# Expert outputs scattered into x itself, with the experts visited in an order that alternates groups

## The chip, the cores and the metric

The kernel runs on one core of a Trainium2 chip. The metric is the device time of one execution in microseconds (us). One profiled execution stands beside the timed runs; every duration in this document is from it.

## The reference, cut to what matters

The model has two layers. Each is a token mixer (gated linear attention in the first, an RG-LRU block in the second) and then a mixture of experts, each added to `x`; a final RMSNorm follows. `x` has 2048 rows (tokens) of 1024 float32 values. There are 32 experts in 4 groups of 8. A token picks one group and then two experts inside it:

```
g_sel = jnp.argmax(grp_logits, axis=-1)
exp_logits = jnp.take_along_axis(exp_logits, g_sel[:, None, None], axis=1)[:, 0]
top_p, top_e = lax.top_k(exp_prob, MOE_TOPK)                  # MOE_TOPK = 2
eid = g_sel[:, None] * MOE_EXPERTS_PER_GROUP + top_e
...
def expert_block(args):
    xblk, e = args
    return (jax.nn.silu(xblk @ w_gate[e]) * (xblk @ w_up[e])) @ w_down[e]
yb = yb * buf_w[:, None].astype(yb.dtype)
out = jnp.zeros((n_tok + 1, d), yb.dtype).at[buf_tok].add(yb)[:n_tok]
```

So each token receives the weighted outputs of two experts of one group. The rows that an expert gets are cut into blocks of 128, the last one padded.

## The kernel before

All five engines run one program, stage after stage: `gla`, `route0` (output projection, residual into the DRAM tensor `x1`, norm, routing, lists of tokens per expert), `experts0`, `lru`, `route1` (the same into `x2`), `experts1`, `finish`. Every float32 matmul is split into a high and a low float32r part (`matmul3`, three matmuls); ScalarE (ACT) makes the high part, VectorE (DVE) the low part, of weights and of activations.

**The expert stages.** The program loops over the 32 experts and, inside, over an expert's blocks (`Fori(0, n)`, n read from a register); g counts blocks over the whole stage. The software pipeline of block g is spread over iterations:

- GpSimd (POOL), L1350 to L1360, in iteration g: gather half 0 of the rows of h for block g+1, store y of the pipeline index g-1, gather half 1 of block g+1, copy a column of the lists. All gathers and scatters are indirect DMAs issued by POOL and go through one queue (q0, "software_dynamic"), and each is preceded by a small copy that names its rows.
- TensorE (PE), `each` from L1526: the gate and up product of block g, first half (12 matmuls); transposes of half 0 of block g+1 (L1497); the second half; transposes of half 1; then `down(g+1)`, which multiplies the activations made one iteration earlier, so y of index i belongs to block i-2; then the transposes of the activation of block g (L1505).
- ACT, L1426: copies the transposed activation (L1388), takes y out of PSUM with the token's weight as scale (L1396, `take_y`), takes half 0 of the next rows (L1383), silu (L1432), half 1.
- DVE, L1480: the low parts of the same (L1461, L1456), and silu times up (L1485).
- Before an expert's first block ACT and DVE split the gate and up weights of expert e+1 (L1404, L1445, four parts) and the down weights of expert e (L1410, L1451). The sync engine (SP) loads 3 MB of weights for each expert two experts ahead (L1290), released by these splits.

There is one buffer `y` and one pair of PSUM banks for it. So `take_y(i)` waits until the scatter of y(i-1) has landed, the scatter of y(i) waits for `take_y(i)`, and `down(i+1)` waits for `take_y(i)`. The scatter writes the 128 rows of y to `y_rows`, a DRAM tensor with two rows per token (and 128 spare rows, the target of padding). Padded slots of a gather read some row of h.

**The stages after.** `lru` first makes x + y_a + y_b for each tile of 128 tokens (`combine`, two DVE adds, L1885 and L1886), stores it back to `x1`, and then takes mean square, root, norm (L1782, L1787, L1890, L1892), transposes and splits. Four tiles are made ahead of its first step, the others one per step. `finish` does the same adds (L2104, L2105) on `x2`, the norm (L2085, L2089, L2107, L2110) and stores to `out`. Their first tiles of x (two and six) are loaded during the expert stage.

## Time and profile before

| | us |
|---|---|
| median of 3 runs | 3018.33 (3016.26 to 3020.65) |
| the profiled execution | 3014.33 |
| its span (first to last instruction) | 3012.6 |
| PE busy | 2619.9 (87%) |
| DVE busy | 1820.9 (60%) |
| ACT busy | 1647.7 (55%) |
| POOL busy | 590.5 (20%) |

The busy times are sums over stages with different limits. PE is marked busy while matmuls are pipelined, so its share says little by itself; the idle time before an instruction, and what ended it, says more. The two expert stages fill about a third of the span. The mean DMA rate over the span is 190 GB/s.

A row of the windows view gives the stretch in us, its length, the busy time and the instruction count of PE, PEld (weight load), DVE, ACT and POOL, the granted TensorE clock as a share of full speed, the DMA engines' busy share, and GB/s. A row of the timeline gives the start, the duration, the engine, the line, the operation, what it writes and reads, and in brackets the idle time of the engine before it and what ended it.

### The profile page before, as it was taken

Reading aid. Unit: us, or ns where it says so; the run is one execution under the profiler, and the core shown is the slowest. Engines: PE = TensorE matmul, PEld = TensorE weight load, DVE = VectorE, ACT = ScalarE, POOL = GpSimd, SP = SyncE. Lnnn points to the kernel's source line nnn. Section 1 sums busy time; section 2 is a strip of 40 time slices with the busy share of each in tenths; the row PEclk is TensorE's granted clock in tenths of the full one; section 3 lists DMA queues with packets and bytes.
Section 4 is the critical chain, followed back from the end, with each engine's and each line's share of the span. In section 5 each row is a group of like instructions: output and inputs, shape, how many; then the busy total and the mean of one; then the engine's idle time right before and its main releaser. Section 6 shows DMA issues by size and latency. Waiting matters only on the chain. (4 is left out here: it accounts for less than half of the span.)

```text
span 3012.6 us, 41660 instructions
## 1 busy us (share of the span) xinstructions
PE 2619.9 (87%) x12246; PEld 2100.4 (70%) x12246; DVE 1820.9 (60%) x3169; ACT 1647.7 (55%) x2260; POOL 590.5 (20%) x795
## 2 busy tenths in 40 slices
PE   6999999999799599999976999999599589999850
PEld 4878878788688477777755777777488467777640
DVE  4555555554456566565636888877465577556546
ACT  5565565554344366565635666675444376555532
POOL 0000000000011344555430000000011255545420
PEclk9999999999899799999987999999799799999985
DMA  3223223331445589789866545451444599877867
GB/s 122 90 91 101 89 91 105 104 107 57 142 155 167 173 295 312 273 281 323 271 218 215 175 166 168 144 171 63 128 154 147 178 350 337 289 264 265 307 237 293
DMA packets 388258, 573.61 MB, mean 190 GB/s; under 512 B 33408, under 2 KB 304000, under 8 KB 384000
## 3 DMA queue, kind: packets, MB, share of 16 engines
q1 hardware_dynamic: 353104, 457.23, 45.8%
q0 software_dynamic: 32688, 105.99, 9.4%
q10 hardware_dynamic: 2304, 8.39, 0.7%
q8 instruction: 81, 1.33, 0.2%
q14 instruction: 81, 0.66, 0.1%
HBM read 449.32 MB, written 122.22 MB: 190 GB/s over the span
## 5 line engine op out<-in xcount | busy, mean ns | idle before, releaser
L1445 DVE TENSOR_TENSOR experts_gu_lo<-carry_raw,experts_gu_hi 128x1024 fp32r<-128x1024 f32 x256 | 296.6, 1220 | 64.4 <-ACT experts_gu_hi L1404 62.4
L1327 POOL DMA_INDIRECT experts_rows<-h_rows,experts_source_now x194 | 269.8, 1391 | 274.0 <-PE experts_ps L1497 129.3
L118 PE MATMUL experts_ps<-experts_gu_hi,experts_hT_hi 128*128 128x512 f32 x760 | 316.3, 416 | 3.0 <-issue 3.0
L119 PE MATMUL experts_ps<-experts_gu_lo,experts_hT_hi 128*128 128x512 f32 x760 | 300.3, 395 | 0.0
L120 PE MATMUL experts_ps<-experts_gu_hi,experts_hT_lo 128*128 128x512 f32 x760 | 299.9, 395 | 0.0
L1404 ACT ACTIVATE experts_gu_hi<-carry_raw 128x1024 fp32r<-128x1024 f32 x256 | 250.2, 1057 | 52.5 <-DMA carry_raw<-in_moe_w_up 42.8
L1456 DVE TENSOR_TENSOR experts_hT_lo<-experts_ps,experts_hT_hi 128x512 fp32r<-128x512 f32 x194 | 133.2, 687 | 240.6 <-ACT experts_hT_hi L1383 233.6
L963 POOL MEMSET route_empty<- 128x512 int32 x2 | 1.1, 564 | 1322.1 <-POOLq L160 1322.1
L118 PE MATMUL route_ps<-route_w_hi,route_src_hi 128*128 128x512 f32 x512 | 208.6, 407 | 45.7 <-DVE route_src_lo L1029 45.7
L1396 ACT ACTIVATE experts_y<-experts_ps,experts_by_block 128x1024 f32<-128x1024 f32 x99 | 110.6, 1117 | 213.8 <-DMA y_rows<-experts_y,experts_target_now 208.4
L119 PE MATMUL route_ps<-route_w_lo,route_src_hi 128*128 128x512 f32 x512 | 203.4, 397 | 0.0
L120 PE MATMUL route_ps<-route_w_hi,route_src_lo 128*128 128x512 f32 x512 | 203.1, 397 | 0.0
L1497 PE MATMUL experts_ps<-ident,experts_rows 128*128 128x128 f32 x776 | 121.1, 279 | 93.4 <-DMA experts_rows<-h_rows,experts_source_now 90.7
L118 PE MATMUL experts_ps<-experts_wd_hi,experts_aT_hi 128*128 (+1 forms) x396 | 172.1, 435 | 26.8 <-DVE experts_aT_lo L1461 22.7
L1497 PEld LDWEIGHTS experts_ps<-ident,experts_rows 128*128 128x128 f32 x776 | 92.8, 142 | 136.1 <-issue 109.9
L120 PEld LDWEIGHTS experts_ps<-experts_gu_hi,experts_hT_lo 128*128 128x128 f32 x760 | 142.6, 188 | 34.6
L118 PEld LDWEIGHTS experts_ps<-experts_gu_hi,experts_hT_hi 128*128 128x128 f32 x760 | 143.0, 188 | 29.6 <-issue 3.5
L119 PE MATMUL experts_ps<-experts_wd_lo,experts_aT_hi 128*128 (+1 forms) x396 | 161.9, 409 | 0.0
L119 PEld LDWEIGHTS experts_ps<-experts_gu_lo,experts_hT_hi 128*128 128x128 f32 x760 | 143.5, 189 | 25.7
L120 PE MATMUL experts_ps<-experts_wd_hi,experts_aT_lo 128*128 (+1 forms) x396 | 161.3, 407 | 0.0
L1451 DVE TENSOR_TENSOR experts_wd_lo<-ahead_wd_raw,experts_wd_hi 128x2048 fp32r<-128x2048 f32 x64 | 146.7, 2293 | 8.3 <-ACT experts_wd_hi L1410 7.0
L975 POOL DMA_INDIRECT expert_lists<-route_entry,route_place_int x64 | 61.7, 964 | 437.1 <-DVE route_place_int L1094 427.3
(322 smaller groups left out, 6757.1 us busy)
## 6 DMA issues: line engine op xcount, KB each, us to landing
carry_raw<-in_moe_w_gate SPq DMA_DIRECT2D x64, 1024.0 KB
carry_raw<-in_moe_w_up SPq DMA_DIRECT2D x64, 1024.0 KB
ahead_wd_raw<-in_moe_w_down SPq DMA_DIRECT2D x64, 1024.0 KB
gla_w_raw<-in_gla_w_in SPq DMA_DIRECT2D x32, 1024.0 KB, 7.3
ahead_wd_raw<-in_lru_w_in SPq DMA_DIRECT2D x32, 1024.0 KB
gla_w_raw<-in_gla_w_in SPq DMA_DIRECT2D x32, 512.0 KB, 5.1
route_src<-oT_rows SPq DMA_DIRECT2D x32, 512.0 KB
x_rows<-route_x_new SPq DMA_DIRECT2D x32, 512.0 KB, 2.9
```

The costliest lines, as they stand in the source:

```text
L118: nc.tensor.matmul(out, w_hi, x_hi, start=first, stop=False)
L119: nc.tensor.matmul(out, w_hi, x_lo, start=False, stop=False)
L120: return nc.tensor.matmul(out, w_lo, x_hi, start=False, stop=last)
L963: pool.memset(empty[:, :, 1], 0)
L975: pool.indirect_dma_start(lists_out, bass.IndirectOffsetOnAxis(place_int[:, j, c:c + 1].bitcast(U32), 0), entry[:, j, c], None).then_inc(s ...
L1327: pool.indirect_dma_start(rows[:, b], None, h_halves[b], bass.IndirectOffsetOnAxis(source_now[b][:].bitcast(U32), 0))\
L1396: nc.scalar.activation(y[:].rearrange("p (b c) -> p b c", b=2), ps[:, Y:Y + 2], ACT.Copy, scale=by_block[:, bass.ds(i + (LAG - 2), 1), 1]. ...
L1404: nc.scalar.activation(gu_hi[:, slot(e), of_part(c)], gu_raw[:, slot(e), of_part(c)], ACT.Copy)\
L1445: nc.vector.tensor_tensor(gu_lo[:, slot(e), of_part(c)], gu_raw[:, slot(e), of_part(c)], gu_hi[:, slot(e), of_part(c)].bitcast(F32), ALU.s ...
L1451: nc.vector.tensor_tensor(wd_lo[:, slot(e)], wd_raw[:, slot(e)], wd_hi[:, slot(e)].bitcast(F32), ALU.subtract).then_inc(wd_lo_done, 1)
L1456: nc.vector.tensor_tensor(hT_lo[:, of_half(b)], ps[:, HT_ + b].rearrange("p (a c) -> p a c", c=P), hT_hi[:, of_half(b)].bitcast(F32), ALU. ...
L1497: last = nc.tensor.transpose(ps[:, HT_ + b, c * P:(c + 1) * P], rows[:, b, c * P:(c + 1) * P], k.ident[:])
```

## The change

The 32 experts are visited as expert 0 of each group, then expert 1 of each group, and so on (`ORDER`), so that blocks that follow one another belong to other groups, or to the same expert, and have no token in common. That allows y to be added into x in DRAM: for each block POOL gathers the block's rows of x1 (or x2) into a new buffer `acc`, DVE computes `y = ps * weight + acc` in one instruction (now DVE's `take_y`; ACT's is gone), and POOL scatters that back over the same rows. `y_rows` no longer exists. The lists hold the token number; padded slots are out of bounds, and the indirect DMAs of all three kinds leave them out. `lru` and `finish` lose their adds, the loads of y and (`lru`) the store of x; they can no longer load x ahead, `finish` has 8 buffers of x and takes the mean square of tile t+1 ahead of the store of tile t.

POOL has two more instructions in an iteration (a copy and a gather) and another order. In the kernel before, this is its order from the start of an iteration; `source_now` names rows of h, `target_now` rows of `y_rows`:

```order
L1321 COPY experts_source_now<-experts_sources 128x1
L1324 REGISTER_ALU
L1325 ISA
L1327 DMA experts_rows<-h_rows,experts_source_now 128x512
L1338 REGISTER_ALU
L1340 ISA
L1340 COPY experts_target_now<-experts_by_block 128x1
L1345 REGISTER_ALU
L1347 DMA y_rows<-experts_y,experts_target_now 4224x1024
L1321 COPY experts_source_now<-experts_sources 128x1
L1325 REGISTER_ALU
L1327 DMA experts_rows<-h_rows,experts_source_now 128x512
```

And this is the same place now; `acc_now` names rows of x, `x_rows` is x1 or x2:

```order
L1369 COPY experts_acc_now<-experts_by_block 128x1
L1358 REGISTER_ALU
L1359 REGISTER_ALU
L1361 DMA x_rows<-experts_y,experts_target_now 2048x1024
L1376 DMA experts_acc<-x_rows,experts_acc_now 128x1024
L1333 ISA
L1333 COPY experts_source_now<-experts_lists 128x1
L1338 REGISTER_ALU
L1340 DMA experts_rows<-h_rows,experts_source_now 128x512
L1333 COPY experts_source_now<-experts_lists 128x1
L1338 REGISTER_ALU
L1340 DMA experts_rows<-h_rows,experts_source_now 128x512
```

The scatter, once between the two gathers of h, stands ahead of both, with the gather of x right behind it.

On DVE the rows from the splits to the end of a first block were, before:

```order
L1445 TENSOR_TENSOR experts_gu_lo<-carry_raw,experts_gu_hi 128x1024 x4
L1451 TENSOR_TENSOR experts_wd_lo<-ahead_wd_raw,experts_wd_hi 128x2048
L1268 UNCONDITIONAL_BRANCH
L1268 ISA
L1461 TENSOR_TENSOR experts_aT_lo<-experts_ps,experts_aT_hi 128x256
L1455 ISA
L1456 TENSOR_TENSOR experts_hT_lo<-experts_ps,experts_hT_hi 128x512
L1485 TENSOR_TENSOR experts_act<-experts_silu,experts_ps 128x256
L1455 REGISTER_ALU
L1456 TENSOR_TENSOR experts_hT_lo<-experts_ps,experts_hT_hi 128x512
```

and are now:

```order
L1470 TENSOR_TENSOR experts_gu_lo<-carry_raw,experts_gu_hi 128x1024 x4
L1476 TENSOR_TENSOR experts_wd_lo<-ahead_wd_raw,experts_wd_hi 128x2048
L1278 UNCONDITIONAL_BRANCH
L1278 ISA
L1486 TENSOR_TENSOR experts_aT_lo<-experts_ps,experts_aT_hi 128x256
L1491 ISA
L1493 REGISTER_ALU
L1495 ISA
L1495 SCALAR_TENSOR_TENSOR experts_y<-experts_ps,experts_by_block,experts_acc 128x1024
L1480 ISA
L1481 TENSOR_TENSOR experts_hT_lo<-experts_ps,experts_hT_hi 128x512
L1522 TENSOR_TENSOR experts_act<-experts_silu,experts_ps 128x256
```

The new instruction on y stands between the low part of the activation and the low part of the next rows.

The diff, cut to its core (`m.sem` and `m.plain` declarations, signatures and the calls are left out):

```diff
+ORDER = [g * EPG + j for j in range(EPG) for g in range(GROUPS)]
...
-                sp.dma_start(into, w[e:e + 1].rearrange("e (k p) c -> p e k c", p=P)).then_inc(landed, DMA)
+                sp.dma_start(into, w[ORDER[e]:ORDER[e] + 1].rearrange("e (k p) c -> p e k c", p=P)).then_inc(landed, DMA)
...
             def gather(b, g):
                 pool.wait_ge(source_set[b], nth(g))
                 pool.wait_ge(hT_ps_done, nth(2 * g - 2 + b))
                 stand(pool)
                 pool.indirect_dma_start(rows[:, b], None, h_halves[b],
-                                        bass.IndirectOffsetOnAxis(source_now[b][:].bitcast(U32), 0))\
+                                        bass.IndirectOffsetOnAxis(source_now[b][:].bitcast(U32), 0),
+                                        bounds_check=T - 1, oob_is_err=False)\
                     .then_inc(rows_in[b], DMA)
...
                 pool.wait_ge(target_set, nth(i + 2))
                 pool.wait_ge(y_done, nth(i))
                 stand(pool)
-                pool.indirect_dma_start(y_rows, bass.IndirectOffsetOnAxis(target_now[:].bitcast(U32), 0),
-                                        y[:], None).then_inc(y_stored, DMA)
+                pool.indirect_dma_start(x_rows, bass.IndirectOffsetOnAxis(target_now[:].bitcast(U32), 0),
+                                        y[:], None, bounds_check=T - 1, oob_is_err=False).then_inc(y_stored, DMA)
+
+            def name_acc(i):
+                if not (isinstance(i, int) and i == -1):
+                    pool.wait_ge(acc_in, nth_acc(i - 1))
+                pool.wait_ge(listed, nth(i - 2))
+                stand(pool)
+                pool.tensor_copy(acc_now[:].unsqueeze(1), by_block[:, bass.ds(i + (LAG - 2), 1), 0:1])\
+                    .then_inc(acc_set, 1)
+
+            def gather_acc(i):
+                pool.wait_ge(acc_set, nth(i + 1))
+                pool.wait_ge(y_done, nth(i - 1))
+                stand(pool)
+                pool.indirect_dma_start(acc[:], None, x_rows,
+                                        bass.IndirectOffsetOnAxis(acc_now[:].bitcast(U32), 0),
+                                        bounds_check=T - 1, oob_is_err=False).then_inc(acc_in, DMA)
 
             def each(e, b, g, n):
-                last = 1 - (n - b + (SLOTS - 2)) // SLOTS
-                column = (e * SLOTS + b + 1 + last * (SLOTS - 1 - b)) % (E * SLOTS)
+                more = (n - b + (SLOTS - 2)) // SLOTS
+                column = more * (b + (ORDER[e] * SLOTS + 1)) + (1 - more) * (ORDER[(e + 1) % E] * SLOTS)
                 column = nc.s_assert_within(column, min_val=0, max_val=E * SLOTS - 1)
+                name_targets(g - 1)
+                name_acc(g)
+                store_y(g - 1)
+                gather_acc(g)
                 name_rows(0, column, g + 1)
                 gather(0, g + 1)
-                name_targets(g - 1)
-                store_y(g - 1)
                 name_rows(1, column, g + 1)
                 gather(1, g + 1)
                 keep_list(column, g + 1)
...
-            def take_y(i):
-                act.wait_ge(y_ps_done, nth(i))
-                act.wait_ge(y_stored, nth_stored(i - 1))
-                act.wait_ge(listed, nth(i - 2))
-                stand(act)
-                nc.scalar.activation(y[:].rearrange("p (b c) -> p b c", b=2), ps[:, Y:Y + 2], ACT.Copy,
-                                     scale=by_block[:, bass.ds(i + (LAG - 2), 1), 1].bitcast(F32))\
-                    .then_inc(y_done, 1)
-
...
+            def take_y(i):
+                dve.wait_ge(y_ps_done, nth(i))
+                dve.wait_ge(acc_in, nth_acc(i))
+                dve.wait_ge(y_stored, nth_stored(i - 1))
+                dve.wait_ge(listed, nth(i - 2))
+                stand(dve)
+                nc.vector.scalar_tensor_tensor(
+                    out=y[:].rearrange("p (b c) -> p b c", b=2), in0=ps[:, Y:Y + 2],
+                    scalar=by_block[:, bass.ds(i + (LAG - 2), 1), 1].bitcast(F32),
...
             def each(e, b, g, n):
                 take_aT(g)
+                take_y(g)
                 take_rows(g + 1, 0)
...
             def load_x(t):
+                after(sp, h_done, t - 2)
                 sp.dma_start(x[:, t % 2], x_dram[t * P:(t + 1) * P, :]).then_inc(x_in[t % 2], DMA)
 
-            def load_y(t):
-                after(sp, x_done, t - 2)
-                sp.dma_start(y_ab[:, t % 2], y_tiles[t]).then_inc(y_in[t % 2], DMA)
-
-            def store_x(t):
-                after(sp, x_done, t)
-                sp.dma_start(x_dram[t * P:(t + 1) * P, :], x[:, t % 2]).then_inc(x_stored[t % 2], DMA)
-
-            def next_x(t):
-                store_x(t - 2)
-                load_y(t)
-                after(sp, h_done, t - 2)
-                after_dma(sp, x_stored[t % 2], t // 2 - 1)
+            for t in range(GT + 2):
                 load_x(t)
-
-            for t in range(2):
-                load_y(t)
-            next_x(2)
-            for t in range(1, GT):
-                next_x(t + 2)
             after(sp, wx["lo_done"], 0)
             load(wx, 1)
             after(sp, wg["lo_done"], 0)
...
-            def combine(t):
-                j = t % 2
-                after_dma(dve, x_in[j], t // 2)
-                after_dma(dve, y_in[j], t // 2)
-                step(nc.vector.tensor_tensor(x[:, j], x[:, j], y_ab[:, j, 0], ALU.add))
-                nc.vector.tensor_tensor(x[:, j], x[:, j], y_ab[:, j, 1], ALU.add).then_inc(x_done, 1)
...
-            combine(0)
             normalise(0)
             for t in range(GT):
-                combine(t + 1)
                 take_hT(t, 2 * (t % 2))
...
                 gated_input(n)
-                if t + 1 < NT:
-                    combine(t + 1)
                 ratio(n)
...
             for t in range(NT):
-                after(sp, x_done, t - DEPTH)
-                sp.dma_start(y_ab[:, t % DEPTH], y_tiles[t]).then_inc(y_in[t % DEPTH], DMA)
-                late = t + XD - DEPTH
-                if t >= DEPTH and late < NT:
-                    after(sp, h_done, late - XD)
-                    sp.dma_start(x[:, late % XD], x_dram[late * P:(late + 1) * P, :])\
-                        .then_inc(early.x_in[late % XD], DMA)
+                after(sp, h_done, t - XD)
+                sp.dma_start(x[:, t % XD], x_dram[t * P:(t + 1) * P, :]).then_inc(x_in[t % XD], DMA)
...
 
         @block.scalar
         def _(act):
-            for t in range(NT):
+            def mean_square(t):
                 j = t % DEPTH
-                after(act, x_done, t)
+                act.wait_ge(x_in[t % XD], (t // XD + 1) * DMA)
                 after(act, std_done, t - 1)
                 nc.scalar.activation(square[:], x[:, t % XD], ACT.Square, accum_out=ss[:, j:j + 1])\
                     .then_inc(ss_done, 1)
+
+            mean_square(0)
+            for t in range(NT):
+                j = t % DEPTH
                 after(act, h_done, t - DEPTH)
                 after(act, ss_done, t)
                 nc.scalar.activation(std[:, j:j + 1], ss[:, j:j + 1], ACT.Sqrt, bias=k.eps[:, 0:1], scale=1.0 / D)\
                     .then_inc(std_done, 1)
+                if t + 1 < NT:
+                    mean_square(t + 1)
                 after(act, h_done, t)
```

## Rows read from the trace of the kernel before

**Rows 1.** Windows: experts0, start of lru, lru, experts1 (stretch, length, busy times, clock, DMA share, GB/s).
```profile
1021.50:1577.20 555.70, 494.77 (x2288) 389.49 (x2288) 326.91 (x363) 319.99 (x412) 266.25 (x362) 0.96 0.81 276
1577.20:1615.50 38.30, 7.83 (x33) 6.29 (x33) 27.40 (x31) 17.78 (x28) 0.00 (x0) 0.50 0.82 300
1615.50:2110.00 494.50, 469.05 (x2016) 375.07 (x2016) 388.00 (x431) 319.33 (x354) 0.00 (x0) 0.98 0.44 147
2400.00:2915.20 515.20, 461.13 (x2143) 361.95 (x2142) 310.89 (x342) 305.23 (x390) 249.02 (x329) 0.98 0.83 289
```
**Rows 2.** One instruction per block (L1485), experts0 and experts1: count, durations, first and last start.
```profile
L1485 DVE TENSOR_TENSOR experts_act<-experts_silu,experts_ps x49: 405/410/422, 1050.0 to 1558.0; 128x256 f32<-128x256 f32 x49
L1485 DVE TENSOR_TENSOR experts_act<-experts_silu,experts_ps x46: 408/410/424, 2414.9 to 2897.2; 128x256 f32<-128x256 f32 x46
```
**Rows 3.** Timeline, all engines, 1203 to 1226 us: start, duration, engine, idle before and releaser.
```profile
1203.05 0.99 POOL L1347 DMA_INDIRECT y_rows<-experts_y,experts_target_now  x1 [0.87 <-POOL experts_target_now L1340]
1205.11 1.00 POOL L1327 DMA_INDIRECT experts_rows<-h_rows,experts_source_now  x1 [0.86 <-POOL experts_source_now L1321]
...
1211.75 1.11 ACT L1396 ACTIVATE experts_y<-experts_ps,experts_by_block 128x1024 f32<-128x1024 f32 x1 [6.14 <-DMA y_rows<-experts_y,experts_target_now]
...
1212.52 0.65 PE L1497 MATMUL experts_ps<-ident,experts_rows 128*128 128x128 f32 x4 [1.27 <-DMA experts_rows<-h_rows,experts_source_now]
1213.17 0.49 PE L118 MATMUL experts_ps<-experts_wd_hi,experts_aT_hi 128*128 x1
...
1219.09 0.60 PE L1497 MATMUL experts_ps<-ident,experts_rows 128*128 128x128 f32 x4
...
1220.48 2.42 POOL L1327 DMA_INDIRECT experts_rows<-h_rows,experts_source_now  x1 [1.84 <-PE experts_ps L1497]
...
1221.96 0.42 DVE L1461 TENSOR_TENSOR experts_aT_lo<-experts_ps,experts_aT_hi 128x256 fp32r<-128x256 f32 x1
...
1222.82 0.49 PE L118 MATMUL experts_ps<-experts_wd_hi,experts_aT_hi 128*128 x1
```
**Rows 4.** Timeline, start of experts0: the first gather and the transposes that wait for it.
```profile
1028.40 1.03 POOL L1327 DMA_INDIRECT experts_rows<-h_rows,experts_source_now  x1 [0.91 <-POOL experts_source_now L1321]
...
1032.06 1.08 PE L1497 MATMUL experts_ps<-ident,experts_rows 128*128 128x128 f32 x4 [19.31 <-DMA experts_rows<-h_rows,experts_source_now]
```
**Rows 5.** One line (L1892): VectorE's instruction on 128x1024 with a scalar and a second tensor, ns.
```profile
L1892 DVE SCALAR_TENSOR_TENSOR lru_h<-lru_early_x,lru_rstd,lru_early_gain x16: 1283/1285/1286, 1587.7 to 1977.3; 128x1024 f32<-128x1024 f32 x16
```
**Rows 6.** Windows inside one expert of two blocks: 1203 to 1213 and 1217 to 1222 us.
```profile
1203.00:1213.00 10.00, 8.73 (x43) 6.76 (x41) 0.81 (x2) 1.64 (x3) 3.73 (x7) 1.00 0.99 350
1217.00:1222.00 5.00, 5.00 (x25) 4.09 (x24) 4.98 (x5) 4.48 (x5) 3.16 (x4) 1.00 0.20 54
```
**Rows 7.** Timeline, start of lru.
```profile
1582.18 1.22 DVE L1885 TENSOR_TENSOR lru_early_x<-lru_early_x,lru_y_ab 128x1024 f32<-128x1024 f32 x1 [4.72 <-DMA lru_y_ab<-y_rows]
...
1606.18 1.06 ACT L1782 ACTIVATE lru_square<-lru_early_x 128x1024 bf16<-128x1024 f32 x1 [1.83 <-DVE lru_early_x L1886]
```
**Rows 8.** Timeline, end of experts1 and finish.
```profile
2902.42 0.98 POOL L1347 DMA_INDIRECT y_rows<-experts_y,experts_target_now  x1 [3.99 <-ACT experts_y L1396]
2906.01 1.11 ACT L1396 ACTIVATE experts_y<-experts_ps,experts_by_block 128x1024 f32<-128x1024 f32 x1 [4.37 <-DMA y_rows<-experts_y,experts_target_now]
...
2915.20 7.79 SPq L2072 DMA_DIRECT2D finish_y_ab<-y_rows  x5
...
2936.30 0.16 DVE L2107 RECIPROCAL finish_rstd<-finish_std 128x1 f32<-128x1 f32 x1 [1.54 <-ACT finish_std L2089]
...
2937.81 0.37 ACTq L2092 DMA_DIRECT2D out<-finish_h  x1
...
2941.39 0.29 ACT L2089 ACTIVATE finish_std<-finish_ss,eps 128x1 f32<-128x1 f32 x1
2941.72 0.17 DVE L2107 RECIPROCAL finish_rstd<-finish_std 128x1 f32<-128x1 f32 x1 [1.54 <-ACT finish_std L2089]
...
3008.98 0.34 ACTq L2092 DMA_DIRECT2D out<-finish_h  x1
```

113 lines of the change are left out of this document (47 added, 66 removed).

## The prediction

> **What bounds the kernel now.** I read the windows by stage first, then the timeline of a few blocks in an expert stage, then the starts of `lru` and `finish`. In the windows the reader sees that the two expert stages take 555.7 and 515.2 us, with PE busy for 494.8 and 461.1, and DMA at 0.81 and 0.83 of its share [rows 1]. PE is the engine that bounds them, nearly. The instruction that runs once per block gives the count and the pace: 49 blocks, (1558.0 - 1050.0) / 48 = 10.58 us each, and 46 blocks, (2897.2 - 2414.9) / 45 = 10.72 us each [rows 2]. With 32 experts that is 17 and 14 experts of two blocks and 33 of one, if none has three. A block without a stall takes 9.65 us, from the first `down` matmul at 1213.17 to the next at 1222.82 [rows 3]. So about 1 us per block is waiting, and the timeline shows on what: the scatter issued at 1203.05 lands only when ACT takes the next y at 1211.75, 8.7 us later, and the gather issued behind it at 1205.11 releases the transposes at 1212.52, 7.4 us later [rows 3]. At the start of the stage, with nothing else in flight, the first gather took 1032.06 - 1028.40 = 3.7 us to the transposes [rows 4]. The long ones coincide with the weights: DMA is at 0.99 of its share from 1203 to 1213 and at 0.20 from 1217 to 1222 [rows 6]. `lru` has PE busy 469 of 494.5 us, behind a start of 38.3 us in which PE does nearly nothing [rows 1]. `finish`, 2915.2 to 3012.6, is a chain of DVE and ACT [rows 8].
>
> **The expert stages.** Parts: ACT loses its instruction on y; DVE gains one of 1.3 us (1.285 for the same form with SBUF operands [rows 5]; its PSUM operand is not shown in this form, so 1.3 to 1.5); POOL gains a copy and a gather; above all, POOL's order changes. Count from the start of a `down`, 1213.17. DVE first finishes the block before, then splits weights for 6.9 us, then the low part of the activation, which ends at 1221.96 + 0.42 = 1222.38, that is +9.2 [rows 3]. Taking y now follows: it ends at +10.55. `down` of the next block, which PE could begin at +9.65, waits for it: 0.9 us for each of 64 experts, 58 us, is what the DVE part alone costs where nothing else is late.
>
> Next, what is queued behind y. POOL's iteration begins with the scatter, which waits for y; then the gather of x; then the first half of h. From the trace two indirect DMAs that follow one another on POOL are 2.06 us apart (1203.05, 1205.11) and the first comes 0.9 us after its release, so the first half of h is issued at 0.9 + 2 x 2.05 = 5.0 us after y. It was issued ahead of the scatter before, so it did not depend on y at all. It is needed one block later, in the middle of the gate and up product; from those transposes to the next `down` PE takes 1222.82 - 1219.09 = 3.75 us. This closes a loop that spans two blocks: 10.55 (down to y) + 5.0 + L (issue to landing) + 3.75 = 19.3 + L, or (19.3 + L) / 2 per block.
>
> L is not shown for this place: three transfers now stand in the queue, the last is the one that matters. From below it is the undisturbed gather [rows 4], 3.7 us: 11.5 us per block. From above it is the gather behind a scatter while weights load, 7.4: 13.35 us per block. The padded slots, of 95 x 128 = 12160 slots all but 8192, are no longer moved, so a third of the indirect traffic goes and the gather of x takes its place; the sum of bytes stays. I take L = 5.2: the gathers of an expert's first block fall mostly into the quiet stretch, those of its second block, and of single-block experts, into the busy one, and less is queued ahead than in the worst row. That is 12.25 us per block against 10.65, the mean of both stages, times 95: +152 us. The bounds are +81 and +257; the first rival below goes under them.
>
> A further reason against a lower L: the gather issued at 1220.48, beside DVE's split of the down weights, kept POOL for 2.42 us instead of 1.00 [rows 3], and for single-block experts scatter and gathers now fall beside the splits.
>
> The new order mixes experts of popular and unpopular groups, so single-block experts, 3 MB of weights for one block of work, come less in a row. At 350 GB/s [rows 6] the weights of an expert (3.15 MB) take 9.0 us and one block's rows of h and y (1.05 MB) 3.0 us, together 12.0, above the 10.65: such a run is bound by DMA before. Spreading it is worth about 1.3 us for some 8 of 33 single blocks: -10 us. Bounds 0 and -40.
>
> At each stage's end y of the last two blocks is taken in turn. Before, the second comes 3.6 us after the first one's scatter is issued (2902.42, 2906.01) [rows 8]; now a gather is issued between them (2.05) and DVE's instruction is longer; with its wake-up +3 us for each of two stages: +6. The memsets of two more buffers lie in the stage's start, beside the load of the lists; nothing.
>
> **lru.** The first adds begin at 1582.18, 4.9 us after the stage's first load at 1577.3, since 1 MB of y comes first [rows 7]. With the load of x alone I take 3.7 as for the undisturbed gather [rows 4]: -1.2; the two adds of tile 0 are on the chain, 2 x 1.22: -2.4. For tiles 1 and 2 the adds lie beside transposes and splits of the tile before; for tile 3 ACT waits 1.83 us for them at 1606.18 [rows 7], and tile 4's adds delay the last split in the same way, 2.4. Start: -8. In the steady part 11 of 16 tiles' adds remain, 2.45 us each, 27 us of DVE; PE idles 25 us there [rows 1], a part of it for DVE. I take -6, bounds 0 and -20. The stores of x and loads of y go, at a DMA share of 0.44: nothing.
>
> **finish.** A tile takes 2941.72 - 2936.30 = 5.42 us [rows 8]. Without adds, and with the mean square ahead, a tile is: reciprocal to store issued 1.51 (2937.81 - 2936.30), the issue 0.37, root 0.29 and its gap: 2.25 us. DMA then moves 1.05 MB per tile, at 350 GB/s 3.0 us, so transfers bound it: 48 us for 16 tiles and 3.6 for the last store (3008.98 to 3012.6): about 51.5 against 97.4, -46. Bounds: -51 if compute sets it, with its start of 8 us (load 3.7, mean square, table load, root, norm), 15 x 2.25 and a tail of 4; -38 if loads and stores mix at 290 GB/s, the mean of an expert stage.
>
> **Sum.** 3014.3 + 152 - 10 + 6 - 14 - 46 = 3102. The median of the runs is 4 us above the profiled execution; I leave that out: 3102, 2.8% slower.
>
> **Rivals.** First, on the other side: the row gathers land in time. It needs L below about 2 + 0.1, since 19.3 + L = 2 x 10.65 at L = 2.0; or POOL being released earlier, because y of an expert's second block, which has no splits in front of it, is taken some 4 us sooner and empty slots make its transfers short. For it: those second blocks hold few rows, and the y wait, 8.7 us, shrinks if it is mostly queueing. Against it: the only undisturbed gather already takes 3.7. Then the expert stages cost 0 to 40 us, say 15, and the sum is 3014.3 + 15 - 64 = 2965 (64 is 10 + 14 + 46 - 6). It decides from where the loop costs less than 64 us: 11.32 us per block, L = 3.35. The Trainium skill (DMA: Bandwidth & Descriptors, Anatomy of one DMA and Queues, rings and completion order) gives an estimate of 2.0 us plus bytes / 436e3, and engines that take turns between queues, so 2.6 us for half of h however busy the weights' queue; by that rule 10.95 us per block and 2979. The rows at 7.4 and 8.7 us [rows 3] speak against it.
>
> Second: everything behind y lands late, as in the busy rows, with 0.5 MB more ahead of the gather of h: L = 7.4 and more, +257 us, 3207. Single-block experts, half of all, would show it.
>
> Third: the DVE term alone, +58, with L hidden and the rest as summed: 3014 + 58 - 64 = 3008, at the edge of no change.
>
> **Chances.** Forecast 0.55; first rival 0.18; second 0.15; third 0.12, of which half is no change and a third is faster. What a measurement can tell from no change is 0.2%, 6 us. Faster 0.18 + 0.04 = 0.22, within 0.06, slower 0.72. The range that holds the time 8 times in 10 reaches from the upper end of the first rival to near the second: 2985 to 3185; the forecast's own is 3040 to 3160.
>
> **What would show it.** In the profile after: the distance between DVE's silu-times-up instructions, 12.2 us on average if right, 10.7 if the first rival holds; PE's L1497 (transposes of h) waiting for the gather of h, 3 to 4 us in most second blocks, 90 us in total before, 200 or more now; `down` waiting for DVE's y about 0.9 us after a split. `finish` at 50 us with tiles 3 us apart, and `lru`'s first product 30 us after its first load. Wrong would be an expert stage no longer than before, or one whose wait is for weights.

## The result, and the profile after

The changed kernel takes 3205.0 us (median of 4 runs, 3198.5 to 3212.2) against 3017.8 of the kernel before on the same chip: a ratio of 1.062, 95% interval 1.0596 to 1.0644. It is 187 us slower. The forecast said 3102 and a range up to 3185: the direction was right, and so was the place, but the cost was double the forecast's 88 us, and the time lies outside the range. The profiled execution took 3212.2 us (span 3210.5), 197.9 more than the one before. The parts below are of these two executions.

First the windows of the changed kernel: experts0, the start of `lru`, `lru`, experts1. The columns are stretch, length, busy times of PE, PEld, DVE, ACT and POOL, the granted clock, DMA share and GB/s.
```profile
1022.00:1700.00 678.00, 526.63 (x2288) 419.91 (x2288) 389.72 (x414) 272.46 (x361) 330.87 (x468) 0.88 0.66 220
1700.00:1740.00 40.00, 14.92 (x53) 11.95 (x54) 17.73 (x26) 18.69 (x29) 0.00 (x0) 0.53 0.45 145
1740.00:2230.00 490.00, 463.01 (x1996) 370.49 (x1994) 360.29 (x404) 320.75 (x356) 0.00 (x0) 0.99 0.34 111
2510.00:3160.00 650.00, 496.01 (x2150) 395.15 (x2150) 375.06 (x395) 264.54 (x347) 308.88 (x432) 0.87 0.66 224
```
Against [rows 1] the expert stages are 100 and more us longer. PE shows as many matmuls in experts0 (2288) but 32 us more busy time, and its clock fell from 0.96 to 0.88. DMA's share fell from 0.81 to 0.66, and the software queue moved 102.87 MB where it moved 105.99: the added time is not a matter of bytes.

The instruction that runs once per block, in both stages (count, durations in ns, first and last start):
```profile
L1522 DVE TENSOR_TENSOR experts_act<-experts_silu,experts_ps x49: 406/420/423, 1063.1 to 1677.8; 128x256 f32<-128x256 f32 x49
L1522 DVE TENSOR_TENSOR experts_act<-experts_silu,experts_ps x46: 405/420/422, 2544.0 to 3134.5; 128x256 f32<-128x256 f32 x46
```
That is 614.7 / 48 = 12.81 and 590.5 / 45 = 13.12 us per block, against 10.58 and 10.72 [rows 2].

The costliest groups whose idle time changed (busy us, mean ns | idle before, releaser). The first row is the kernel before, the others are the changed kernel:
```profile
L1497 PE MATMUL experts_ps<-ident,experts_rows 128*128 128x128 f32 x776 | 121.1, 279 | 93.4 <-DMA experts_rows<-h_rows,experts_source_now 90.7
...
L1536 PE MATMUL experts_ps<-ident,experts_rows 128*128 128x128 f32 x776 | 138.0, 307 | 258.4 <-DMA experts_rows<-h_rows,experts_source_now 258.4
L120 PE MATMUL experts_ps<-experts_gu_hi,experts_hT_hi 128*128 128x512 f32 x760 | 347.9, 458 | 1.2 <-issue 1.2
...
L1495 DVE SCALAR_TENSOR_TENSOR experts_y<-experts_ps,experts_by_block,experts_acc 128x1024 f32<-128x1024 f32 x99 | 126.7, 1279 | 170.7 <-DMA experts_acc<-x_rows,experts_acc_now 163.0
L120 PE MATMUL experts_ps<-experts_wd_hi,experts_aT_hi 128*128 (+1 forms) x396 | 167.8, 424 | 45.4 <-DVE experts_y L1495 45.4
...
L1361 POOL DMA_INDIRECT x_rows<-experts_y,experts_target_now x103 | 106.4, 1033 | 339.8 <-DVE experts_y L1495 336.0
```
POOL stands at the scatter for 336 us until DVE has y; behind it wait the gathers of h; and PE idles 258 us before the transposes of h, where it was 90.7 before. All but 2 us of the 258 are waits for half 0; before, 49 us were for half 0 and 42 for half 1. `down` waits 45 us for DVE's y, where it waited 26.8 in all.

The table adds up the difference. "First" and "last" are the first and last start of the per-block instruction; the loads are SP's first of `lru` and `finish`.

| part | before | after | difference | forecast |
|---|---|---|---|---|
| both stages, first to last block | 990.3 | 1205.2 | +214.9 | +152 - 10 |
| up to the first block of experts0 | 1050.0 | 1063.1 | +13.1 | 0 |
| experts1, from its first transposes of the activation to its first block | 11.0 | 23.6 | +12.6 | 0 |
| last block to the next stage's first load | 19.3 + 18.0 | 25.1 + 28.0 | +15.8 | +6 |
| `lru`, first load to first product | 38.2 | 30.0 | -8.2 | -8 |
| from there to experts1's first transposes of the activation | 788.4 | 787.5 | -0.9 | -6 |
| `finish`, first load to end | 97.4 | 48.0 | -49.4 | -46 |
| sum | | | +197.9 | +88 |

Now one pair of blocks in the timeline of the changed kernel (start, duration, engine, idle before and releaser):
```profile
1331.77 0.49 PE L120 MATMUL experts_ps<-experts_wd_hi,experts_aT_hi 128*128 x1 [1.00 <-DVE experts_y L1495]
...
1332.35 1.02 POOL L1361 DMA_INDIRECT x_rows<-experts_y,experts_target_now  x1 [4.69 <-DVE experts_y L1495]
...
1333.68 1.03 POOL L1376 DMA_INDIRECT experts_acc<-x_rows,experts_acc_now  x1 [0.31 <-issue]
...
1335.84 1.05 POOL L1340 DMA_INDIRECT experts_rows<-h_rows,experts_source_now  x1 [0.92 <-issue]
...
1341.46 1.28 DVE L1495 SCALAR_TENSOR_TENSOR experts_y<-experts_ps,experts_by_block,experts_acc 128x1024 f32<-128x1024 f32 x1 [5.57 <-DMA experts_acc<-x_rows,experts_acc_now]
1342.39 1.11 PE L1536 MATMUL experts_ps<-ident,experts_rows 128*128 128x128 f32 x4 [4.62 <-DMA experts_rows<-h_rows,experts_source_now]
...
1344.58 0.63 PE L120 MATMUL experts_ps<-experts_gu_hi,experts_hT_hi 128*128 128x512 f32 x1
...
1348.81 0.48 PE L120 MATMUL experts_ps<-experts_wd_hi,experts_aT_hi 128*128 x1
...
1357.88 1.27 DVE L1495 SCALAR_TENSOR_TENSOR experts_y<-experts_ps,experts_by_block,experts_acc 128x1024 f32<-128x1024 f32 x1
1359.46 0.50 PE L120 MATMUL experts_ps<-experts_wd_hi,experts_aT_hi 128*128 x1 [1.02 <-DVE experts_y L1495]
```
The predicted loop is there (`down`, y, gather of half 0 of h behind the scatter and the gather of x, transposes, the next `down`), and its four legs can be read. `down` to the end of y: 1359.15 - 1348.81 = 10.3. End of y to the issue of half 0, from the y before the first `down`, which ended at 1330.19 + 1.27: 4.4. Issue to transposes, 1335.84 to 1342.39: L = 6.55. Transposes to `down`, 1342.39 to 1348.81: 6.4. Together 27.7 us for two blocks, where 24.5 was forecast; most of both stages runs in such pairs, 10.5 and then 16 to 17.7 us from block to block. The pair is a typical one: PE waits over 2 us for half 0 at 41 places, and over these the median of L is 6.6 us and that of the leg from transposes to `down` 5.9. From one such wait to the next are two blocks 24 times, at a median of 27.8 us, and three blocks 12 times, at 36.9, where a block without a wait (9.4) lies between. One leg was missed altogether: in this pair PE took 6.4 us from the transposes to `down`, and not 3.75. Windows of that stretch show why (clock in the third column from the end):
```profile
1331.70:1341.70 10.00, 6.01 (x26) 4.60 (x26) 1.96 (x5) 0.38 (x1) 5.09 (x9) 1.00 1.00 352
1342.30:1348.40 6.10, 6.01 (x16) 4.77 (x17) 1.13 (x2) 0.60 (x1) 3.49 (x5) 0.50 0.47 142
```
After 4.62 us without work PE is granted the lower of its two levels, 1.2 GHz, for these 6 us: its matmuls last 0.63 us and not 0.39.

What the two parts, waiting and clock, are in the stages can be read from windows that reach from first to last block, two of the kernel before and two of the changed one:
```profile
1050.00:1558.00 508.00, 474.55 (x2214) 374.53 (x2213) 307.56 (x345) 302.59 (x392) 250.20 (x337) 0.99 0.85 290
2414.90:2897.20 482.30, 444.11 (x2075) 349.46 (x2074) 300.77 (x332) 293.65 (x377) 240.30 (x316) 0.99 0.86 299
```
```profile
1063.10:1677.80 614.70, 503.83 (x2210) 402.39 (x2209) 366.63 (x391) 257.98 (x345) 305.32 (x430) 0.90 0.69 231
2544.00:3134.50 590.50, 471.51 (x2072) 376.53 (x2071) 355.86 (x376) 251.76 (x332) 283.76 (x400) 0.89 0.68 233
```
Of the +214.9 us, PE stands idle for 158 more (229.9 for 71.7), and is busy for 57 more with the same matmuls. The waits are the larger part; the increase in busy time is the clock's, as far as busy times tell.

The start of experts0 in the timeline, first of the kernel before, then of the changed one, and last the same place in experts1:
```profile
1045.51 0.65 PE L1497 MATMUL experts_ps<-ident,experts_rows 128*128 128x128 f32 x4 [1.60 <-DMA experts_rows<-h_rows,experts_source_now]
```
```profile
1043.76 1.26 POOL L1361 DMA_INDIRECT x_rows<-experts_y,experts_target_now  x1 [0.73 <-POOL experts_acc_now L1369]
1045.33 1.97 POOL L1376 DMA_INDIRECT experts_acc<-x_rows,experts_acc_now  x1 [0.31 <-issue]
...
1049.58 1.04 POOL L1340 DMA_INDIRECT experts_rows<-h_rows,experts_source_now  x1 [0.94 <-POOL experts_source_now L1333]
...
1056.96 1.11 PE L1536 MATMUL experts_ps<-ident,experts_rows 128*128 128x128 f32 x4 [13.26 <-DMA experts_rows<-h_rows,experts_source_now]
...
2537.34 1.11 PE L1536 MATMUL experts_ps<-ident,experts_rows 128*128 128x128 f32 x4 [13.25 <-DMA experts_rows<-h_rows,experts_source_now]
```
The gather of h for the second block is issued behind a scatter and a gather of x; PE waits 13.26 us for it, where it waited 1.60, and 13.25 us in experts1.

And the end of experts1, where the last two y follow one another:
```profile
3142.88 1.01 POOL L1361 DMA_INDIRECT x_rows<-experts_y,experts_target_now  x1 [4.59 <-DVE experts_y L1495]
...
3144.99 1.04 POOL L1376 DMA_INDIRECT experts_acc<-x_rows,experts_acc_now  x1 [0.90 <-POOL experts_acc_now L1369]
...
3149.34 1.28 DVE L1495 SCALAR_TENSOR_TENSOR experts_y<-experts_ps,experts_by_block,experts_acc 128x1024 f32<-128x1024 f32 x1 [7.34 <-DMA experts_acc<-x_rows,experts_acc_now]
3151.49 1.01 POOL L1361 DMA_INDIRECT x_rows<-experts_y,experts_target_now  x1 [5.10 <-DVE experts_y L1495]
3162.52 0.34 SPq L2050 DMA_DIRECT2D finish_x<-x_rows  x1
```
Between these two scatters lie 8.6 us, since y now waits for the landing of old x: it starts 6.5 us after the scatter, where ACT's y came 3.6 us after it [rows 8]. The end has a second part, which the rows above do not show: once its last scatter has landed, POOL runs a DRAIN before the next stage may begin. Its durations at the end of experts0 (min/median/max in ns, of a stretch that holds that one and a short one of 40), before and then now:
```profile
L158 POOLq DRAIN  x2: 40/1766/3492, 1572.8 to 1577.3; - x2
```
```profile
L160 POOLq DRAIN  x2: 40/3932/7825, 1694.0 to 1702.9; - x2
```
It takes 7.83 us and not 3.49, and at the end of experts1 6.84 and not 2.76: 8.4 us more in both. All kernels below that gather x in a stage have the long one at its end (6.8 to 7.8 us), all others, e3 too, the short one. Why is open.

`finish`, one tile to the next, and the last store:
```profile
3175.49 0.36 ACTq L2073 DMA_DIRECT2D out<-finish_h  x1
...
3177.74 0.36 ACTq L2073 DMA_DIRECT2D out<-finish_h  x1
...
3206.57 0.34 ACTq L2073 DMA_DIRECT2D out<-finish_h  x1
```
A tile takes 2.25 us here, and 2.37 on the mean of the 15 steps from the first store at 3170.95 to the last, where it took 5.42 [rows 8].

### The profile page after: what moved, and what is told of

It reads as the page before. It is cut to its first block and busy times, and to the rows that moved or that the text cites. A ratio compares the mean times of both kernels' runs of the same rounds, so it can differ in the third digit from the quotient of the medians.

```text
span 3210.5 us, 42505 instructions
## 1 busy us (share of the span) xinstructions
PE 2686.6 (84%) x12246; PEld 2164.0 (67%) x12246; DVE 1867.2 (58%) x3204; ACT 1555.5 (48%) x2161; POOL 712.2 (22%) x1001
## 3 DMA queue, kind: packets, MB, share of 16 engines
q0 software_dynamic: 47232, 102.87, 9.2%
q8 instruction: 81, 1.33, 0.2%
## 5 line engine op out<-in xcount | busy, mean ns | idle before, releaser
L120 PE MATMUL experts_ps<-experts_gu_hi,experts_hT_hi 128*128 128x512 f32 x760 | 347.9, 458 | 1.2 <-issue 1.2
L121 PE MATMUL experts_ps<-experts_gu_lo,experts_hT_hi 128*128 128x512 f32 x760 | 325.2, 428 | 0.0
L122 PE MATMUL experts_ps<-experts_gu_hi,experts_hT_lo 128*128 128x512 f32 x760 | 324.8, 427 | 0.0
L1420 ACT ACTIVATE experts_hT_hi<-experts_ps 128x512 fp32r<-128x512 f32 x194 | 115.8, 597 | 354.6 <-PE experts_ps L1536 354.5
L1340 POOL DMA_INDIRECT experts_rows<-h_rows,experts_source_now x194 | 229.4, 1182 | 192.5 <-POOL experts_source_now L1333 115.1
L1495 DVE SCALAR_TENSOR_TENSOR experts_y<-experts_ps,experts_by_block,experts_acc 128x1024 f32<-128x1024 f32 x99 | 126.7, 1279 | 170.7 <-DMA experts_acc<-x_rows,experts_acc_now 163.0
L120 PEld LDWEIGHTS experts_ps<-experts_gu_hi,experts_hT_hi 128*128 128x128 f32 x760 | 163.6, 215 | 30.9 <-issue 1.6
L121 PEld LDWEIGHTS experts_ps<-experts_gu_lo,experts_hT_hi 128*128 128x128 f32 x760 | 162.9, 214 | 30.0
L1361 POOL DMA_INDIRECT x_rows<-experts_y,experts_target_now x103 | 106.4, 1033 | 339.8 <-DVE experts_y L1495 336.0
L1459 ACT ACTIVATE experts_silu<-experts_ps 128x256 f32<-128x256 f32 x95 | 36.5, 384 | 276.8 <-PE experts_ps L122 270.1
```

The lines of the kernel that those rows point to most:

```text
L120: nc.tensor.matmul(out, w_hi, x_hi, start=first, stop=False)
L121: nc.tensor.matmul(out, w_hi, x_lo, start=False, stop=False)
L122: return nc.tensor.matmul(out, w_lo, x_hi, start=False, stop=last)
L1340: pool.indirect_dma_start(rows[:, b], None, h_halves[b], bass.IndirectOffsetOnAxis(source_now[b][:].bitcast(U32), 0), bounds_check=T - 1, ...
L1361: pool.indirect_dma_start(x_rows, bass.IndirectOffsetOnAxis(target_now[:].bitcast(U32), 0), y[:], None, bounds_check=T - 1, oob_is_err=Fal ...
L1420: nc.scalar.activation(hT_hi[:, of_half(b)], ps[:, HT_ + b].rearrange("p (a c) -> p a c", c=P), ACT.Copy).then_inc(hT_hi_done, 1)
```

## The experiments

The theory: the time is lost because POOL's gather of half 0 of h stands behind y, with the clock's fall on top. The rivals: the gather of x as such (one more transfer, and y waiting for it), the work on DVE, the bound on the row numbers, the order of the experts. Each kernel was timed against the kernel before in the same batch, and batches differ by up to 4 us, so kernels of different batches are compared by their ratios. In the summary, "stages" is both expert stages, first to last block, and the rest is all other time; both are differences of one profiled execution each to that of before, so a few us of them are scatter (e4 shows +8 us in its execution and nothing in its median).

| kernel | median us | ratio to before, 95% | stages | rest | clock |
|---|---|---|---|---|---|
| after | 3205.0 | 1.0620 [1.0596, 1.0644] | +214.9 | -17.0 | 0.916 |
| e1_half0_first | 3068.0 | 1.0151 [1.0131, 1.0171] | +85.3 | -27.6 | 0.937 |
| e2_both_first | 3231.4 | 1.0694 [1.0676, 1.0712] | +242.6 | -22.9 | 0.913 |
| e3_no_acc_gather | 3108.1 | 1.0294 [1.0277, 1.0311] | +146.1 | -52.5 | 0.933 |
| e8_filler | 3174.9 | 1.0521 [1.0504, 1.0539] | +179.9 | -19.4 | 0.956 |
| e6_acc_ahead | 3049.3 | 1.0109 [1.0092, 1.0126] | +77.6 | -41.9 | 0.948 |
| e4_order_alone | 3018.0 | 1.0006 [0.9997, 1.0016] | +7.5 | +0.6 | 0.943 |
| e5_scatter_first | 3071.7 | 1.0183 [1.0166, 1.0200] | +47.6 | +11.1 | 0.937 |
| e7_y_on_dve | 3028.8 | 1.0047 [1.0032, 1.0061] | +5.2 | +6.7 | 0.945 |
| e9_names_first | 3084.9 | 1.0214 [1.0196, 1.0231] | +107.7 | -35.4 | 0.943 |
| e10_skip_empty | 3031.0 | 1.0047 [1.0030, 1.0064] | +9.3 | +5.3 | 0.946 |
| e11_sum_last_only | 3010.0 | 0.9984 [0.9974, 0.9994] | +32.3 | -41.5 | 0.952 |

**e1_half0_first**, the changed kernel with one gather moved back:
```diff
+                name_rows(0, column, g + 1)
+                gather(0, g + 1)
                 name_targets(g - 1)
                 name_acc(g)
                 store_y(g - 1)
                 gather_acc(g)
-                name_rows(0, column, g + 1)
-                gather(0, g + 1)
```


> The changed kernel, but GpSimd gathers half 0 of the next rows of h ahead of the scatter of y, as before; scatter, gather of x and half 1 follow. Theory (place in GpSimd's order: the gathers of h wait for y): the transposes of half 0 no longer wait about 5 us in every second block, the pace falls from 12.96 us per block to about 11.3, set by the y cycle of scatter, gather of x and VectorE; about 3050 us. Rival (the queue is simply longer with the gather of x in it): the gathers land late wherever they stand, half 1 stalls instead, over 3150 us.

Measured 3068.0, 18 us above the expected 3050: 137 of the 187 us go. The place of one gather is most of the loss. What stays is seen in two groups of its trace, first PE at the transposes, then DVE at y:
```profile
  DMA experts_rows<-h_rows,experts_source_now: 159.7, 62
```
```profile
L1495 DVE SCALAR_TENSOR_TENSOR experts_y<-experts_ps,experts_by_block,experts_acc 128x1024 f32<-128x1024 f32 x99 | 126.8, 1281 | 217.6 <-DMA experts_acc<-x_rows,experts_acc_now 217.4
```
PE waits 160 us for rows of h (258 before the edit), and DVE now 217 for the gather of x (163 before the edit). Told apart by half, the wait for half 0 fell from 256 us to 54, about what it is in the kernel before (49), and that for half 1, which still stands behind y, rose from 2 to 106 (42 in the kernel before). So the theory holds for half 0, and in a small part the rival too: half 1 stalls instead.

**e2_both_first**: both gathers of h ahead of the scatter.
```diff
+                name_rows(0, column, g + 1)
+                gather(0, g + 1)
+                name_rows(1, column, g + 1)
+                gather(1, g + 1)
                 name_targets(g - 1)
                 name_acc(g)
                 store_y(g - 1)
                 gather_acc(g)
-                name_rows(0, column, g + 1)
-                gather(0, g + 1)
-                name_rows(1, column, g + 1)
-                gather(1, g + 1)
```


> The changed kernel, but both halves of the next rows of h are gathered ahead of the scatter of y. Theory (place): neither half waits for y, but the scatter now waits for the transposes that free half 1's buffer, so y comes later than with half 0 alone ahead: between 3030 and 3090 us. Rival (queue length): over 3150 us.

Measured 3231.4, slower than the changed kernel: a miss. The wait only changed its owner. Its `down` (idle before, releaser), and POOL's gathers of h:
```profile
L120 PE MATMUL experts_ps<-experts_wd_hi,experts_aT_hi 128*128 (+1 forms) x396 | 203.4, 514 | 286.3 <-DVE experts_y L1495 286.2 <-issue 0.2
```
```profile
L1340 POOL DMA_INDIRECT experts_rows<-h_rows,experts_source_now x194 | 202.8, 1045 | 425.6 <-PE experts_ps L1536 350.0 <-POOL experts_source_now L1333 55.8 <-issue 10.0
```
The gathers of h wait 350 us for the transposes that free their buffers; the scatter and the gather of x stand behind them; y comes late, and `down` waits 286 us for y. POOL issues in program order, so what is released first has to stand first.

**e3_no_acc_gather**: no gather of old x.
```diff
-                name_acc(g)
                 store_y(g - 1)
-                gather_acc(g)
```


> The changed kernel without the gather of x (the old rows of x are left out of the sum; everything else stays, the scatter still first). Theory (place): y to the gather of half 0 shortens by one indirect DMA's issue, 1.3 us, and its landing by the data ahead of it, about 1 us, so 2.3 us per two blocks: about 3100 us, and the transposes still wait for rows that were issued after y. Rival (queue length and the wait for the gather of x are the cost): 3000 us or less.

The old rows of x are left out of the sum, so the second layer works on other values and routes its tokens otherwise: experts1 still has 46 blocks, but not the same number per expert. experts0 has the same blocks.

Measured 3108.1, as the theory had it (3100). The gather of x as such, in the changed order, is worth 97 us of the 187 (29 us in experts0, where the work is the same: +77.6 for +106.7). Without it the stages are still 146 us longer than before. The landing did not get quicker, against what was expected: at the 40 waits of over 2 us the median of L is 6.7 us, and with the gather of x ahead it was 6.6. What is queued just ahead does not set L; what does was not tested, beyond that the weights load at that time.

**e8_filler**: the changed kernel with twelve matmuls per block into a bank that nobody reads, ahead of the transposes that wait.
```diff
+                        for c in range(4):
+                            matmul3(nc, ps[:, 6], hT_hi[:, c], hT_lo[:, c], gu_hi[:, slot(e), c],
+                                    gu_lo[:, slot(e), c], c == 0, c == 3)
```


> The changed kernel with 12 matmuls more per block on TensorE (2.8 us, into an unused PSUM bank), between the first half of the gate and up product and the transposes that wait for the rows. Theory (a part of the cost is TensorE's clock, which the trace shows at half speed for some 5 us after each wait of 5 us): the wait shrinks to 2 us, the clock holds, and although PE has 266 us of work more over both expert stages the kernel gets faster, by 60 to 120 us. Rival (only the wait itself costs): same or slower, up to +60 us.

Measured 3174.9: 30 us faster, though 1140 matmuls are added, which at 0.23 us from one to the next (the pace at the full clock) are some 260 us of work. The expected 60 to 120 was too much. Windows of both stages, first of this kernel, then of the changed one without the filler:
```profile
1066.00:1668.00 602.00, 587.62 (x2787) 477.11 (x2785) 371.26 (x391) 259.97 (x343) 294.20 (x426) 1.00 0.71 236
2540.00:3102.00 562.00, 543.49 (x2580) 441.87 (x2579) 353.23 (x370) 247.56 (x325) 281.85 (x399) 1.00 0.72 246
```
```profile
1066.00:1668.00 602.00, 494.05 (x2170) 394.75 (x2169) 363.54 (x387) 256.40 (x340) 299.39 (x418) 0.90 0.69 232
2546.00:3134.00 588.00, 469.01 (x2059) 374.43 (x2058) 354.26 (x374) 249.36 (x328) 282.09 (x398) 0.89 0.68 234
```
The clock is back at 1.00. The 36 pairs of blocks that hold a long wait in the changed kernel take 25.3 us here on the mean, and 27.5 there. With the filler a block is at least 12.1 us of PE's own work, so a pair can't be under 24.2: the run shows that the loop at the full clock is no longer than 25.3 us, and so that the clock is 2.2 us or more of each pair. The gain of 82 us in these pairs is for the most part lost again in the other 21 blocks, which go from 10.2 to 12.4 us on the mean (+47 us). These 82 us are more than the 57 by which PE's busy time rose, so the clock's share of the stages is known only to that: some 60 to 80 us of the 215.

**e4_order_alone**: the kernel before, experts in the new order.
```diff
+ORDER = [g * EPG + j for j in range(EPG) for g in range(GROUPS)]
...
-                n = (words[e // PACK] // PACK_BASE ** (e % PACK)) % PACK_BASE
+                at = ORDER[e]
+                n = (words[at // PACK] // PACK_BASE ** (at % PACK)) % PACK_BASE
```


> The kernel before with the new order of experts alone. Theory: single-block experts come less in a row, DMA-bound runs go, -10 us or less: 3005 to 3018 us. Rival (order has no part): within 4 us of before.

Measured 3018.0 at a ratio of 1.0006 [0.9997, 1.0016]: no difference that can be told. The forecast's -10 was nothing.

**e5_scatter_first**: the kernel before, with the scatter ahead of the gather of half 0, and nothing else.
```diff
-                name_rows(0, column, g + 1)
-                gather(0, g + 1)
                 name_targets(g - 1)
                 store_y(g - 1)
+                name_rows(0, column, g + 1)
+                gather(0, g + 1)
```


> The kernel before with GpSimd's scatter of y ahead of the gather of half 0, the one change in its order; no gather of x. Theory (place in the order): every second block waits 3 to 4 us for rows of h, plus the clock: the loop is 10.35 - 1.3 (y on ScalarE is no later than that) + 3 + 5.5 + 4 to 6.4, 22 to 24 us per two blocks against 21.3: 3060 to 3130 us. Rival: without the gather of x there is no such wait, within 20 us of before.

Measured 3071.7, in the range of the theory: the place alone, without a gather of x and with y on ACT, costs 57 us. Its transposes wait in sum as e1's do, but for half 0 (146 us), as in the changed kernel, and not for half 1 (11 us):
```profile
  DMA experts_rows<-h_rows,experts_source_now: 157.0, 59
```

**e7_y_on_dve**: the kernel before, `take_y` on VectorE instead of ScalarE, behind the low part of the activation as in the changed kernel.
```diff
-                nc.scalar.activation(y[:].rearrange("p (b c) -> p b c", b=2), ps[:, Y:Y + 2], ACT.Copy,
-                                     scale=by_block[:, bass.ds(i + (LAG - 2), 1), 1].bitcast(F32))\
-                    .then_inc(y_done, 1)
...
+                nc.vector.tensor_scalar(y[:].rearrange("p (b c) -> p b c", b=2), ps[:, Y:Y + 2],
+                                        by_block[:, bass.ds(i + (LAG - 2), 1), 1].bitcast(F32), None,
+                                        ALU.mult).then_inc(y_done, 1)
```


> The kernel before with y taken out of PSUM and weighted on VectorE in place of ScalarE. Theory (the VectorE term of the prediction): +0.9 us per expert, 58 us, since the split of the next weights stands ahead of it and TensorE's down product waits: 3060 to 3080 us. Rival (hidden behind other waits in the second blocks): 3015 to 3035 us.

Measured 3028.8, 14 us: the rival. `down` waits for y as forecast, but it had waited before too, for the low part of the activation. Its row, before and then here:
```profile
L118 PE MATMUL experts_ps<-experts_wd_hi,experts_aT_hi 128*128 (+1 forms) x396 | 172.1, 435 | 26.8 <-DVE experts_aT_lo L1461 22.7
```
```profile
L118 PE MATMUL experts_ps<-experts_wd_hi,experts_aT_hi 128*128 (+1 forms) x396 | 173.6, 438 | 46.0 <-DVE experts_y L1457 43.8 <-issue 1.3
```
So the wait ahead of `down` grows by 19 us and not by 58. The rows of h, half 0 of which does not wait for y here, take 16 of these back: PE waits 74 us for them where it waited 91. The stages are 5.2 us longer. Together with e5 and e3 this shows that the parts do not add: the place alone +47.6 in the stages, y on DVE alone +5.2, both (e3) +146.1, both and the gather of x +214.9.

**e6_acc_ahead**: the order of e1, and old x gathered a block ahead into a second buffer that ACT copies (the order below is the whole change in POOL's loop; the copy and its semaphore are left out).
```diff
+                name_rows(0, column, g + 1)
+                gather(0, g + 1)
                 name_targets(g - 1)
-                name_acc(g)
                 store_y(g - 1)
-                gather_acc(g)
-                name_rows(0, column, g + 1)
-                gather(0, g + 1)
                 name_rows(1, column, g + 1)
                 gather(1, g + 1)
+                name_acc(g + 1)
+                gather_acc(g + 1)
```


> The changed kernel with half 0 of h ahead of the scatter, and the gather of x moved off the cycle of y: it is issued one block earlier, behind half 1, into a second buffer that ScalarE copies (1.06 us per block) to the one VectorE adds. Theory (what is left after half 0 is ahead is the wait for the gather of x, inside the cycle scatter, gather, VectorE): the waits of y for x vanish, only the scatter's landing is left, the pace falls to 10.6 to 11.0 us per block and the gain at the start of lru and in finish comes through: 2975 to 3010 us, faster than before. Rival (a fourth indirect transfer in the queue delays all of them while weights load): 3050 us or more.

Measured 3049.3: better than e1 by 13 us by the ratios, but not below the kernel before; a miss. Its transposes wait as long as e1's in sum, but in more and shorter waits (1.7 us each for 2.6):
```profile
  DMA experts_rows<-h_rows,experts_source_now: 155.6, 91
```
The clock is 0.948 for e1's 0.937, which fits the shorter waits; it was not tested apart.
POOL now has four transfers per block in a row and its last one waits for a copy that follows y:
```profile
L1378 POOL DMA_INDIRECT experts_acc_raw<-x_rows,experts_acc_now x99 | 107.4, 1085 | 230.4 <-ACT experts_acc L1433 190.8 <-POOL experts_acc_now L1370 33.9 <-issue 3.5
```

**e9_names_first**: e6 with the index copies a transfer earlier.
```diff
                 name_rows(0, column, g + 1)
+                name_targets(g - 1)
                 gather(0, g + 1)
-                name_targets(g - 1)
                 store_y(g - 1)
                 name_rows(1, column, g + 1)
+                name_acc(g + 1)
                 gather(1, g + 1)
-                name_acc(g + 1)
                 gather_acc(g + 1)
```


> As e6_acc_ahead (ratio 1.0109), but the two index copies of GpSimd that stood between two transfers stand one transfer earlier (the scatter's index ahead of the gather of half 0, that of the gather of x ahead of the gather of half 1), so that two of the four transfers of a block follow the one before them after 1.3 us in place of 2.2. Theory: what is left of the loss in the expert stages is GpSimd's row of four transfers, 0.9 us dearer where a copy stands between; about 30 of the 96 blocks wait on it, twice 0.9 us each at most: 20 to 50 us faster than e6, 3000 to 3030. Rival: the copies now wait for the landing of the transfer before last (they overwrite the index that it reads), and hold back the gathers behind them; the same as e6 or slower, 3045 or more.

Measured 3084.9, 32 us slower than e6 by the ratios: the rival. The copy of the index of x, in e6 and then here:
```profile
L1370 POOL COPY experts_acc_now<-experts_by_block 128x1 int32 (+1 forms) x99 | 45.0, 455 | 3.4 <-DMA experts_acc_raw<-x_rows,experts_acc_now 2.8 <-issue 0.5
```
```profile
L1370 POOL COPY experts_acc_now<-experts_by_block 128x1 int32 (+1 forms) x99 | 41.2, 416 | 116.8 <-DMA experts_acc_raw<-x_rows,experts_acc_now 115.2 <-issue 1.4
```
Moved ahead of a gather of h it waits 115 us for a landing in place of 3, and holds that gather back. The copy of the scatter's index waits 46 us for 5. Whether the 0.9 us between two transfers matter at all is not told apart by this run.

**e10_skip_empty**: e7 with the bound on the gathers of h (the row numbers of empty places are also no longer masked into the range, which the cut leaves out).
```diff
-                                        bass.IndirectOffsetOnAxis(source_now[b][:].bitcast(U32), 0))\
+                                        bass.IndirectOffsetOnAxis(source_now[b][:].bitcast(U32), 0),
+                                        bounds_check=T - 1, oob_is_err=False)\
```


> As e7_y_on_dve (before, with y taken on VectorE, ratio 1.0047), and the gathers of h skip the empty places of a block by the bound, as the changed kernel does, in place of fetching some row for them. Theory: skipping costs nothing and saves little, since a gather is paid by its latency and not by its bytes: within 6 us of e7, 3023 to 3035. Rival: the bound makes GpSimd's descriptors dearer (its gathers took 1.05 us with it and 1.00 without) and the empty half-full blocks no cheaper: 10 to 25 us slower than e7. Other side: fewer bytes in the queue give 10 us or more back.

Measured 3031.0, ratio 1.0047 [1.0030, 1.0064], as e7's: the software queue moves 89.72 MB for 105.99, and skipping the empty places costs nothing and brings nothing beyond the 5 us that this comparison can tell.

**e11_sum_last_only**: before's experts0 and `lru` (with the new order of experts), e6's experts1 and the new `finish`. The calls, against the kernel before:
```diff
-            early = FinishEarly(nc, held)
-            experts(nc, k, "experts1", h_halves, lists, moe_w_gate[1], moe_w_up[1], moe_w_down[1], y_rows, ahead,
-                    lambda sp, _: early.load(sp, x2, final_norm))
-            finish(nc, k, x2, y_rows, early, out[0])
+            experts_sum(nc, k, "experts1", h_halves, lists, moe_w_gate[1], moe_w_up[1], moe_w_down[1], x2, ahead,
+                        lambda sp, _: None)
+        finish(nc, k, x2, final_norm, out[0])
```


> Before (with the order of the change) in experts0 and lru: y is stored by row number and added in lru. In experts1 and finish the form of e6_acc_ahead: old rows of x gathered a block ahead, sum scattered to x2, finish without rows of y. Theory: the price and the gain of e6 are local. Its experts1 took 531.9 us against 495.9 from the first block's transposes to the last's (+36.0), its end 70.1 against 112.8 (-42.7), and lru gave back only 3: so this one ends at -7, 3005 to 3015, ratio 0.996 to 1.000. Rival: the end's gain depends on lru or experts0 also being changed, or the stage's price is larger when the first stage is not: 3020 or more.

Measured 3010.0 us, ratio 0.9984 [0.9974, 0.9994] over 10 runs: as forecast, and the one version here that comes out below both kernels, by 0.16%, which is at the edge of what can be told. Its experts1 costs 29 us and the rest gives 41. The sum in x pays here only at `finish`, where the adds were on the chain; in `lru` they were on it at the start alone (-8.2).

## Why the prediction was right in direction and wrong in size

**Right.** The loop over two blocks, y to scatter to gather of x to gather of half 0 to transposes to `down`, is in the trace leg by leg, and e1 and e5 show it by experiment: one gather moved back takes 137 us off, and moved behind the scatter in the kernel before it costs 57. It is not the bytes (they fell) nor the bound (e10). `finish` was -49.4 for -46 forecast, with 2.25 us per tile: close to the bound by compute that the prediction named, not the 3.0 us by DMA that it took, so the -46 is in part luck. The bounds come to -52 and -36 from their own terms (8 + 15 x 2.25 + 4, and 16 tiles of 1.05 MB at 290 GB/s + 3.6), not -51 and -38. The start of `lru` was -8.2 for -8.

**The step that failed is the size of the loop term**, "I take L = 5.2", and "from those transposes to the next `down` PE takes 3.75 us". In the pair shown L is 6.55, +1.35; the last leg is 6.4, +2.65, as PE comes out of a wait of 4.6 us with its clock at 0.50; the leg from y to the gather is 4.4 and not 5.0, as two transfers without an index copy between them are 1.33 us apart (1332.35, 1333.68) and not 2.05. In sum 27.7 for 24.5. The leg was read from a stretch in which PE had not waited; a wait that I forecast to be 3 to 4 us had to be followed by a stretch like the slow ones after it. e8 bounds this term: with PE kept busy the pairs take 25.3 us and not 27.5, so the clock is 2.2 us of each or more.

A second error lies in the same term and went the other way. The sum took every block as part of the loop, at half its period. PE waits 52 times in 95 blocks, and 12 of the stretches between long waits hold a third block of 9.4 us, so +3.2 us per pair became +0.7 per block on the mean, 63 us of the 73 by which the stages missed. The other 10 is the order of the experts. Of the 110 us between 88 and 197.9, the stages are 73, the starts 26, the ends 10, and the rest 1.

**The first rival**, the gathers landing in time, needed L below 3.35; the median is 6.6. The fit of the Trainium skill (DMA: Bandwidth & Descriptors, Anatomy of one DMA), 2.0 us plus the bytes at 436 GB/s, gives 2.6 us as an estimate for the 256 KB of half of h. The trace does not agree where the gather runs beside weights at a DMA share of 1.00, with 6.55.

**The order of the experts**, -10: nothing (e4).

**The third rival**, "the DVE term alone, 58": e7 shows 14. The term was counted from a `down` that PE could begin at once. But `down` waited before as well, 26.8 us in all, so DVE's y adds 19, and where half 0 is issued ahead of the scatter 16 of these are won back at the transposes. Inside the loop the same delay costs far more: e3 stands 98.5 us above e5 in the stages (49 of them in experts0, where both do the same work), and what differs is y on DVE, besides the order of the experts (e4) and the bound (e10), neither of which cost anything by itself. So the term was wrong by itself and right as a leg of the loop.

**The starts**, taken as nothing, are +25.7: waits of 13.26 and 13.25 us at the first blocks, 11.7 more each than before, that the prediction, which said only that memsets are hidden, did not look for, although the same row of POOL's queue that makes the loop makes it.

**The ends**, +6, were +15.8. Up to the issue of the last scatter the two ends together are 8.6 us longer: the gather between the last two y was counted by its issue, 2.05 us, and y waits for its landing. The other 7.2 lie behind that scatter, where POOL's DRAIN takes 8.4 us more in both stages; the prediction has no term for it.

**`lru`'s steady part**, -6, was -0.9, in its bounds: PE idles 27.0 us in 490.0 there and 25.5 in 494.5 before [rows 1], so the adds had been hidden.

The range went up to 3185 because the case "everything behind y lands late" got 15%; its 3207 is close to the 3205 measured by chance, as L is 6.6 and not 7.4 or more, and the clock, the starts and the ends make up the rest.

Open: what is left in e6, +77.6 in the stages. The gather as a fourth transfer and y's place in the loop are both in it; e9, meant to part them, added a wait of its own. Gathering old x into two buffers in turn was not tried.

## What to carry to other kernels

Where an engine issues its transfers in program order, a transfer that depends on nothing recent must stay ahead of one that waits for the newest result; when a change inserts a wait, list what stands behind it and follow the circle until it closes, and then count every leg at the clock that PE has after the wait. Count as well which blocks are in the circle at all. A wait that feeds back into itself can cost a multiple of the same delay outside the loop (here 5 us alone, 98 inside). Count a transfer by its landing wherever its result is read next.

## What was not expected of the hardware

- PE after 4.62 us without work: granted clock 0.50 in the 6.1 us that follow, matmuls of 128x512 at 0.63 us and not 0.39. Twelve matmuls of no use ahead of each such wait hold the stage at 1.00 and make the kernel 30 us faster.
- An indirect transfer behind another on POOL is issued 1.33 us after it if its index is ready, and about 2.1 us after it with an index copy between them (1335.84, 1338.00: 2.16).
- Out-of-bound places that a gather skips change nothing that can be measured: 1.0047 with and without, though 16 MB fewer move.
- Half of h (256 KB) takes 6.6 us from issue to its waiter beside the weights, whether a gather of 512 KB stands just ahead of it (after) or not (e3, 6.7).
- POOL's DRAIN at the end of a stage takes 2.8 to 3.5 us in the kernels without the gather of x and 6.8 to 7.8 with it, the same to 0.1 us in every kernel.
